# A two-layer transformer block pair in fp32: how the chunked time mix scan carries its state, and how the gate's 32 inner units are projected

## What is computed

```python
xr, xw, xk, xv, xa, xg = [x + xx * mu[i] for i in range(6)]
...
g = jax.nn.sigmoid(xg @ g1) @ g2          # g1 is 1024 x 160: 160 inner units
...
def step(S, inp):                         # one token, one 64 x 64 state a head
    r_t, d_t, k_t, v_t, a_t, b_t = inp
    sa = jnp.einsum('bhij,bhj->bhi', S, a_t)
    S = (S * d_t[:, :, None, :] + sa[..., None] * b_t[:, :, None, :]
         + v_t[..., None] * k_t[:, :, None, :])
    return S, jnp.einsum('bhij,bhj->bhi', S, r_t)
```

## Time and profile before

| | before |
|---|---|
| median of three runs | 2301.28 us |
| the profiled execution's own time | 2304.67 us |
| its span, first to last instruction | 2302.9 us |
| time mix layer with its start, from the page's and the trace's times | 0 to about 541 us |
| busy share of the span: TensorE, its weight loads, VectorE, ScalarE | 97%, 65%, 48%, 32% |
| mean granted TensorE clock, as a share of full | 0.986 |

### The profile page before, as it was taken

The page is one execution under the profiler, slowest core; times in us unless marked ns, Lnnn a source line. Parts: engine busy times, 40 slices in busy tenths (PEclk is TensorE's granted clock), DMA queues, the critical chain, the costliest instruction groups (busy, mean ns, idle before and its releaser), DMA issues.

```text
span 2302.9 us, 36365 instructions
## 1 busy us (share of the span) xinstructions
PE 2234.3 (97%) x14174; PEld 1485.5 (65%) x14174; DVE 1113.8 (48%) x2661; ACT 729.2 (32%) x1655; POOL 5.3 (0%) x13
## 2 busy tenths in 40 slices
PE   7999999999999999999999999999999999999997
PEld 3555555556688888865486888888646554444553
DVE  7444444442766663254337666524370772213442
ACT  2433433422333320145432333102210552114541
POOL 0000000000000000000000000000000000000000
PEclk9999999998999999999999999999899999999998
DMA  3100000003222222211112222420331111221012
GB/s 108 63 33 33 33 33 33 20 20 129 73 75 90 91 93 95 87 34 40 55 56 91 91 88 76 128 101 37 101 96 59 38 37 55 73 73 46 29 38 73
DMA packets 23210, 151.13 MB, mean 66 GB/s; under 512 B 2624, under 2 KB 2752, under 8 KB 9248
## 3 DMA queue, kind: packets, MB, share of 16 engines
q1 hardware_dynamic: 22032, 145.54, 17.6%
q0 software_dynamic: 1040, 3.64, 1.1%
HBM read 146.58 MB, written 2.59 MB: 65 GB/s over the span
## 4 chain that ended last, share of the span: by engine, by line
PE 94%; DVE 4%; issue 1%; ACT 1%; DMA 0%; SPq 0%; DVEq 0%; ACTq 0%
PE banks L1935 19%; PE banks L1396 12%; PE banks L1268 7%; PE banks L1196 6%; PE banks L2425 5%; PE banks L1315 3%; PE banks L2277 3%; PE banks L515 3%; PE banks L483 3%; PE banks L505 3%; PE banks L1238 2%; PE banks L1905 2%; PE banks L2311 2%; PE banks L617 2%; PE banks L2289 2%; PE banks L3026 2%
## 5 line engine op out<-in xcount | busy, mean ns | idle before, releaser
L1935 PE MATMUL banks<-arena 128*128 128x256 f32 x2016 | 436.4, 379 | 0.0
L1935 PEld LDWEIGHTS banks<-arena 128*128 128x128 f32 x2016 | 382.5, 190 | 54.5 <-issue 1.0
L1396 PE MATMUL banks<-arena 128*128 128x256 f32 x1232 | 267.5, 378 | 0.0
L1396 PEld LDWEIGHTS banks<-arena 128*128 128x128 f32 x1232 | 232.6, 189 | 33.2
L1268 PE MATMUL banks<-arena 128*128 128x512 f32 x384 | 170.3, 601 | 0.0
L1990 ACT ACTIVATE arena<-banks 128x256 f32<-128x256 f32 x180 | 69.2, 385 | 297.2 <-PE banks L1935 297.2
L2150 DVE SCALAR_TENSOR_TENSOR arena<-arena 128x511 f32<-128x511 f32 (+1 forms) x144 | 108.2, 751 | 74.9 <-ACT arena L1999 57.7
L2346 ACT ACTIVATE arena<-arena 128x128 f32<-128x128 f32 (+3 forms) x192 | 101.5, 530 | 122.0 <-DVE arena L2378 121.8
L1196 PE MATMUL banks<-arena 128*128 128x512 f32 x320 | 138.4, 593 | 0.0
L2378 DVE CUSTOM_DVE_ANT_0 arena<-banks,arena 128x256 f32<-128x256 f32 (+3 forms) x160 | 70.8, 472 | 131.4 <-PE banks L2277 130.7
L1268 PEld LDWEIGHTS banks<-arena 128*128 128x128 f32 x384 | 72.8, 192 | 93.1 <-issue 91.0
(11 more groups left out here) (323 smaller groups left out, 3210.0 us busy)
## 6 DMA issues: line engine op xcount, KB each, us to landing
arena<-up SPq DMA_DIRECT2D x44, 1024.0 KB, 4.8
arena<-down SPq DMA_DIRECT2D x16, 1408.0 KB, 6.2
arena<-w_mix SPq DMA_DIRECT2D x8, 1728.0 KB, 7.0
arena<-e_in SPq DMA_DIRECT2D x12, 1024.0 KB, 4.9
arena<-o_in SPq DMA_DIRECT2D x8, 1024.0 KB, 4.7
arena<-w_o SPq DMA_DIRECT2D x4, 1024.0 KB, 5.0
arena<-q SPq DMA_DIRECT2D x8, 512.0 KB, 3.2
arena<-o_attn SPq DMA_DIRECT2D x4, 1024.0 KB, 4.8
```

Of the source, the lines that this page charges most:

```text
L1396: ins = pe.matmul(ps[:, bank, LO], w[:, t, :], x[:, t, :], start=first and t == 0, stop=t == last, skip_group_check=not first)
L1935: ins = pe.matmul(out, w[:, q, :], x[:, q, :], start=start and q == 0, stop=q == 3, skip_group_check=not start)
```

## The change

In the scan, u is no longer found chunk by chunk from a right side that holds the state. Both parts of it are solved for all chunks ahead: X = Z A' (what the state's part turns into) and U0 = Z (K V) (the part without a state). From X come, again for all chunks, one 64x64 matrix M that takes a state on to the next, and one R that takes a state to y. What is left in the chain is, for each chunk, M S added to a sum that already lies in PSUM, one scaling by VectorE, and R S added to y.

- `sides_tensor` (new, in place of the fill after `first`): 8 chunks of a turned A (two antidiagonal quadrants) and of K V (two diagonal ones). ScalarE copies both in level 1 (`sides_scalar`).
- In the last level's second half, and in the scan's first block, `unknowns_tensor`: Z times both sides at once, 128 columns, for 4 chunks each. ScalarE copies each (`unknowns_scalar`).
- In the scan: `to_state` for all chunks (64 rows, 128 columns), to whose result VectorE adds the unit matrix and R (`m`, `r`); the K V sums of all chunks in one PSUM bank ("keys"), the V part of y in another ("side"), B U0 on top ("first"). Then the chain over chunks 1 to 7.
- Gone are for each chunk the copies of rhs and u, ScalarE's faded state, and one fill. The scan now has 15 places for a dense matmul: four between and behind the blocks, then one or two behind each chunk (two next to each other four times). One dense matmul moves from the levels to the opening.
- `gate_tensor` puts the last 32 inner units in four column strips of 32: strip q sums k-tiles q and q+4. ScalarE copies the 128 rows, and one matmul with a stack of four 32x32 unit matrices (`fold_tensor`) adds the strips, two dense steps later.

```diff
+        for i in range(2):
+            for q in range(4):
+                o = KT * P + (4 * i + q) * 32
+                ins = pe.matmul(ps[32 * q:32 * q + 32, 2, :], k.ring[1][:, o:o + 32], self.xg[:, 4 * i + q, :], start=i == 0,
+                                stop=i == 1, tile_position=(0, 32 * q))
...
+    def fold_tensor(self, pe):
+        pe.wait_ge(self.hid_act, 2)
+        pe.wait_ge(self.masks_loaded, 16)
+        self.start_pe.done(pe.matmul(self.k.ps[0:32, 2, :], self.k.const(CR_AT, "fold"), self.hg1, start=True, stop=True), "gate")
...
-                pe.wait_ge(V.sem, V.at(n, f"X{lv}_0"))
+            pe.wait_ge(V.sem, V.at(n, f"X{lv}_0" if lv < LAST else f"Z{lv}_0"))
             laid(lv, 1)
+            if lv == LAST:
+                pe.wait_ge(A.sem, A.at(n, "rhs"))
             for i in range(4):
                 ...
+                if lv == LAST:
+                    found = self.unknowns_tensor(pe, i)
...
+    def sides_tensor(self, pe, n):
+        pe.wait_ge(V.sem, V.at(n, "gram_k1"))
+        pe.wait_ge(self.turned_act.sem, self.turned_act.at(n, "V"))
+        for c in range(NC):
+            cols = slice(c * CH, c * CH + CH)
+            for rows, other in self.PLACES:
+                turned = pe.matmul(ps[other, 5, cols], ar[rows, c, 0:CH], self.eye[rows], start=True, stop=True)
+            for rows, other in self.PLACES:
+                rhs = pe.matmul(ps[other, 7, cols], self.ga[other, c, 3, :], vt[other, c, :], start=True, stop=True)
+    def unknowns_tensor(self, pe, c):
+        for rows, other in self.PLACES:
+            ins = pe.matmul(self.k.ps[rows, c // 4, c % 4 * P:c % 4 * P + P], self.zo[other, c, :], self.at0[other, c, :],
+                            start=True, stop=True)
...
+        def to_state(c):
+            for rows in self.HEADS:
+                ins = pe.matmul(ps[rows, c // 4, c % 4 * P:c % 4 * P + P], self.xu[rows, c, 0:CH],
+                                ga[rows, c, 1:3, :].rearrange("p w t -> p (w t)"), start=True, stop=True)
+        fill(0)
+        pe.wait_ge(L.sem, L.at(n, f"Z{LAST}_1"))
+        pe.wait_ge(A.sem, A.at(n, "xu0"))
+        for i in range(4):
+            found = self.unknowns_tensor(pe, 4 + i)
+            ins = to_state(i)
+        fill(1)
+        pe.wait_ge(A.sem, A.at(n, "xu1"))
+        for i in range(4):
+            for c in (2 * i, 2 * i + 1):
                 for rows, other in self.PLACES:
+                    found = pe.matmul(ps[rows, 2, at(c)], kt[other, c, :], vt[other, c, :], start=c == 0, stop=True, ...)
+            ins = to_state(4 + i)
+        fill(2)
+        for c in range(NC):
             for rows, other in self.PLACES:
+                side = pe.matmul(ps[rows, 7, at(c)], vt[other, c, :], ga[other, c, 4, :], start=c == 0, stop=True, ...)
+            for rows in self.HEADS:
+                ins = pe.matmul(ps[rows, 2, at(c)], ga[rows, c, 1, :], self.xu[rows, c, CH:P], start=False, stop=True, ...)
+        fill(3)
+        i = 4
+        for c in range(1, NC):
+            state = self.s[c % 2]
+            pe.wait_ge(V.sem, V.at(n, f"state{c}"))
+            if c < NC - 1:
                 for rows in self.HEADS:
+                    ins = pe.matmul(ps[rows, 2, at(c)], self.mr[rows, c, 0:CH], state[rows], start=False, stop=True, ...)
+                S.done(ins, f"state{c}")
+            for b in (0, 1) if c == 1 else (c,):
                 for rows in self.HEADS:
+                    ins = pe.matmul(ps[rows, 7, at(b)], self.xu[rows, b, CH:P], ga[rows, b, 2, :], start=False, stop=True, ...)
             for rows in self.HEADS:
+                ins = pe.matmul(ps[rows, 7, at(c)], state[rows], self.mr[rows, c, CH:P], start=False, stop=True, ...)
+            for _ in range(1 if c in (1, 3, 7) else 2):
+                fill(i)
+                i += 1
...
+        for g in range(2):
+            dve.wait_ge(S.sem, S.at(n, f"mr{g}"))
+            V.done(dve.tensor_tensor(self.mr[:, c, 0:CH], found[:, :, 0, :], eye, ALU.add), f"m{g}")
+            V.done(dve.tensor_tensor(self.mr[:, c, CH:P], found[:, :, 1, :], ar[:, c, CH:P], ALU.add), f"r{g}")
+            fill(1 + g)
+        for c in range(1, NC):
+            dve.wait_ge(S.sem, S.at(n, f"state{c - 1}" if c > 1 else "first"))
+            V.done(dve.tensor_scalar(self.s[c % 2], ps[:, 2, c * CH - CH:c * CH], self.last[:, c - 1:c], None, ALU.mult), f"state{c}")
+            fill(2 + c)
...
-            self.early_scalar(act, n + 1, ["w", "a", "blend", "decayed", "grown"])
+            for g, names in enumerate((["w"], ["a"])):
+                self.early_scalar(act, n + 1, names)
+                self.unknowns_scalar(act, n, g)
+            self.early_scalar(act, n + 1, ["blend", "decayed", "grown", "key_root", "r", "v", "g"])
```

More of the change, by code:

```diff
@@ L271 @@
              + [f"Z{LAST}_0", f"Z{LAST}_1"])
-SCAN_PE = [f"{w}{c}" for c in range(NC) for w in (("rhs", "u", "side", "state", "y") if c < NC - 1 else ("rhs", "u", "side", "y"))]
-SCAN_ACT = [f"faded{c}" for c in range(1, NC - 1)]
-SCAN_DVE = ["lasts"] + [f"{w}{c}" for c in range(NC) for w in (("rhs", "u", "state") if c < NC - 1 else ("rhs", "u"))]
+SCAN_PE = ["xu0", "xu1", "mr0", "keys", "mr1", "side", "first"] + [f"state{c}" for c in range(1, NC - 1)] + ["y"]
+SCAN_ACT = ["xu0", "xu1"]
+SCAN_DVE = ["lasts", "m0", "r0", "m1", "r1"] + [f"state{c}" for c in range(1, NC)]
 TAIL_PE = ["var", "spread"]
@@ L308, in __init__ @@
         self.tail_dve = Steps(k.sem("mix_tail_dve"), TAIL_DVE)
[L309 removed]
+        self.start_pe = Steps(k.sem("start_pe"), ["sum", "spread", "hidden", "parts", "gate"])
         self.start_act = Steps(k.sem("start_act"), START_ACT)
@@ L679, in scan_tensor @@
-            fill(2 * c)
-            pe.wait_ge(V.sem, V.at(n, f"rhs{c}"))
-            if c == 0:
-                pe.wait_ge(L.sem, L.at(n, f"Z{LAST}_1"))
-            for rows, other in self.PLACES:
-                ins = pe.matmul(ps[rows, 1, 0:CH], self.zo[other, c, :], self.rhs[other], start=True, stop=True)
-            S.done(ins, f"u{c}")
-            if more:
-                inputs(c + 1)
-                for rows, other in self.PLACES:
-                    pe.matmul(ps[rows, 2, 0:CH], kt[other, c, :], vt[other, c, :], start=True, stop=False)
@@ L690, in scan_tensor @@
-            for rows, other in self.PLACES:
-                ins = pe.matmul(ps[rows, 7, cols], vt[other, c, :], ga[other, c, P + CH:256], start=True, stop=False)
-            S.done(ins, f"side{c}")
-            pe.wait_ge(V.sem, V.at(n, f"u{c}"))
-            pe.wait_ge(S.sem, S.at(n, f"side{c}"))
-            if more:
+            for rows, other in self.PLACES:
+                turned = pe.matmul(ps[other, 5, cols], ar[rows, c, 0:CH], self.eye[rows], start=True, stop=True)
+            for rows, other in self.PLACES:
+                rhs = pe.matmul(ps[other, 7, cols], self.ga[other, c, 3, :], vt[other, c, :], start=True, stop=True)
@@ L702, in scan_tensor @@
             for rows in self.HEADS:
-                ins = pe.matmul(ps[rows, 7, cols], self.u[rows], ga[rows, c, CH:P], start=False, stop=True)
-            S.done(ins, f"y{c}")
-            fill(2 * c + 1)
+                ins = pe.matmul(ps[rows, 7, at(c)], state[rows], self.mr[rows, c, CH:P], start=False, stop=True,
+                                skip_group_check=True)
+            if c == NC - 1:
+                S.done(ins, "y")
+            for _ in range(1 if c in (1, 3, 7) else 2):
+                fill(i)
+                i += 1
```

176 lines of the change are left out of this document (91 added, 85 removed).

## The result

The kernel after takes 2266.84 us (median; 2266.25 to 2267.8), beside 2304.41 for the kernel before on the same chip: ratio 0.984, 95% interval 0.981 to 0.986. Forecast were 2255.8 with a range of 2246 to 2268. So faster, inside the range, but 1.6% instead of 2.0%. The sum was made against one profiled execution, and so is the comparison here: 2304.67 for before (span 2302.9), 2266.25 for after (span 2264.4). That is 38.4 us where the sum had 45.5. The missing 7.1 us are what the experiments look for. (The forecast total is off by 11.0; the other 4.0 come from the medians, which lie 3.4 under the profiled execution in the base of the forecast and 0.6 over it in the kernel after.)

A forecast was written before the change was run, and what follows sets the result against it. TensorE's own queue was taken as the bound, the scan by its chain of small steps. Seven pairs 36.5, last pair 5.0 and gate strips 4.0 sum to 45.5 us off 2301.28: 2255.8 us, range 2246 to 2268.

The forecast's parts named there:

- Start, -4.0: Gate before pair 0: four column strips side by side take 1.9 us for 7.00, the fold 1.0; 4.0 us saved.
- The rival of strips in a row: Gate: the strips do not run side by side, +5.1 us, total 2261; chance 6%.
- The steady scan, -5.91: Last level's second half to next pair's bonus matmul: shorter small parts and adjacent fills save 5.91 us a pair.
- Half B: Last level's second half, with the first four unknowns: 4 chunks x 2 records, 0.93 us with its edge.
- The 0.113: Price in us of one 128-column record with all four quadrants busy, used for the scan's blocks.
- the opening: Start of a pair: dense matmul moved there +0.86 us, sides in its old place; net +0.70 us a pair.
- Seven pairs alike: Bonus matmul to bonus matmul: each of seven pairs saves 5.21 us, 36.5 in all; period 50.9 us.
- Last pair, -5.0: Last pair, last level's second half to last y: 20.45 us for 25.48, 5.0 saved, its opening unchanged.
- What follows is untouched: Everything behind the time mix: unchanged by the change, only starting earlier.
- Turns: Scan blocks: quadrants of a block take turns, 4.2 us a pair, 34 in all, total 2290; chance 5%.
- chain: Scan: each chunk still waits for VectorE's state, up to 4.9 us a pair, total about 2291; chance 4%.
- The slower one: Scan: granted clock falls to half level in every pair, 66 us more, total 2322; chance 3%.

The follow-up runs named there:

- the strips alone: The kernel before with only the gate's four column strips and their fold added, the scan left old: 2302.45 us, ratio 1.001.

## Why the prediction was right, and where its size was off

The mechanism came as forecast: the chain's copies and waits are gone, and the pairs are shorter for it. That the time lies inside the range is partly luck. It is 1.2 us under the upper end, and the largest part of the miss, 4.8 us in two pairs, has a cause that the spread did not contain.

- **Start, -4.0: right.** Strips 1.86 us for 1.9, fold 0.98 for 1.0, the same 1.46 before L568, 3.97 in all. L568 came at 71.84 for 72.4; 0.6 of this lies before the first strip and is not the change's. The rival of strips in a row is out. The estimate from the Trainium skill (TensorE: Matmul & The Clock Gate, "Part 3: Packing small matmuls — row/col tiling"), 3.2 times for four strips, was too careful here: 7.00 / 1.86 is 3.8 times. The time that goes with it, 0.3 us more, did not come.
- **The steady scan, -5.91 by the sum: the term that was mis-sized.** Half B to the next bonus matmul is 24.63 us for 24.37. Half B took 1.04 for 0.93, block 1 1.04 for 0.93, block 3 1.09 for 1.03; block 2 1.13 for 1.15, chunks as forecast. The 0.113 came from the Grams, which other 64x64 tiles follow at once. A block lies between dense matmuls: in block 1 the first records take 0.16 to the next start where the later ones take 0.11, and the last ones 0.20. With the opening (+0.80 for +0.70: `first` and sides took 1.66 for 1.55) the pair got 4.82 less for 5.21; seven pairs, 2.7 us of the 7.1.
- **"Seven pairs alike": failed, 4.8 us.** Pair 0 saved 1.37 and pair 2 3.50. The prediction moved nothing in the slab's request and so did not look at it. But the change packs more records into the time in which the slab's packets run (119 to 143 for 88 to 90). TensorE's instructions are themselves fetched, and it stood still for them 2.33 and 1.07 us. In pair 0 the clock then fell. The runs with the slab moved show this. The kernel before had lost some 1.4 us of its own in pair 0 to its early low stretch (56.82, and 55.46 with the strips alone, which lacks it), else the 1.37 would be nearly nothing.
- **Last pair, -5.0: right in the scan** (half B to last y 20.68 for 20.45), and 1.2 us better behind it, where the low clock cost less.
- **"What follows is untouched": not quite.** A wait for w_o that the trace of before doesn't have cost 1.16; the low clock over L1286 ended sooner, 11.44 us for 12.61, which gave about as much. Some 0.9 us more lie behind, two steps of 0.3 of it near 978 and 1438 us; not settled.
- **Rivals.** Turns, chain and strips one after the other are excluded, by the block's 1.04, the 0.15 us wait and the 1.86. The slower one, a clock that falls in every pair, didn't come: 1.00 in six of the first seven pairs, with four stretches of about 1 us of small matmuls in each. The fall that came followed a standstill of 2.33 us. That the clock holds over the old pairs, the argument against this rival, is not without exception: pair 4 of the strips alone has 0.97.

In sum: 2.7 (sizes) + 3.45 and 1.3 (pairs 0 and 2, beyond the sizes) + 0.9 behind, less 0.6 at the start and 0.9 in the last pair, is 6.9 of the 7.1 us.

## What to carry to other kernels

When a change lets an engine issue more instructions in the same time, look where its instruction packets come from and what large transfer runs then; here moving one request by 18 dense matmuls was worth about 6 us. Write small matmuls of different quadrants in alternation, and keep the large ones together: each change of form costs about 0.1 us on either side here. Work taken from one stretch brings everything behind it forward, so check the next loads too: with its gaps filled the tail ran into a wait of 3.11 us for w_o.

## What the runs showed of the hardware

- TensorE's instructions come in 16 KB packets by the same DMA engines as the data. Behind a 1728 KB transfer such a packet came 1.6 to 3.1 us late in the three cases measured in time; TensorE stood still 0.3 to 2.3 us, in the trace as "issue", or not at all, and went on 2.3 to 2.5 us after the packet's start.
- Five standstills of 2.29 to 2.33 us were followed, 0.4 to 1.7 us after TensorE resumed, by the lower level, for 6.8 us in four traces and 3.4 in one; those of 1.76 and 1.88 in another run by 3.4 us each; the nine of 0.34 to 1.29 by none.
- Four column strips of 32 ran 3.8 times as fast as the same matmuls in one strip. Matmuls for a free quadrant start ahead of earlier ones for a busy quadrant, but only a few (six records in the block): one kind after the other gave 1.53 us where alternation gave 1.04.
